# Recurrence over head pairs: the next pair's preparation and projection interleaved with this pair's matrices and scan, key norms per token, modulation on column groups

## The reference

```python
def rwkv_prep(u, p):
    r, k, v, xw, xa, xg = jnp.split(u, RW_SPLITS, axis=-1)
    w_raw = p['rw_w0'] + jnp.einsum('blde,def->bldf', jnp.tanh(xw), p['rw_w2'])
    decay = jnp.exp(-jnp.exp(-jax.nn.softplus(-w_raw) - 0.5))
    a = jax.nn.sigmoid(p['rw_a0'] + jnp.einsum('blde,def->bldf', xa, p['rw_a2']))
    kk = (k * p['rw_kk']).reshape(b_, n, RW_HEADS, RW_HEAD)
    kk = kk * lax.rsqrt(jnp.maximum(jnp.sum(kk * kk, axis=-1, keepdims=True), 1e-12))
    k_eff = k[:, :, None] * (1 + (a - 1) * p['rw_ka'])

def step(s, inp):
    sa = jnp.einsum('bhvk,bhk->bhv', s, -kk_t)
    s = s * w_t[:, :, None, :] + sa[..., None] * (kk_t * a_t)[:, :, None, :] + v_t[..., None] * k_t[:, :, None, :]
    return s, jnp.einsum('bhvk,bhk->bhv', s, r_t)
```

## Time and profile before

| | us |
|---|---|
| median of 3 runs | 4669.05 (4668.78 to 4669.14) |
| the profiled execution's own time | 4672.97 |
| its span | 4671.2 |
| busy PE / DVE / ACT | 3689.4 / 1769.3 / 776.1 |
| start of the first core stage (L696) | 222.8 |
| start of the last pair's core stage (L696) | 1319.9 |

### The profile page before, as it was taken

One profiled execution on the slowest core, in us unless ns is written; L12 is line 12 of the kernel. 1 busy time (PEld: TensorE's weight loads), 2 busy tenths in 40 slices (PEclk: granted clock), 3 DMA queues, 4 the chain that ended last, 5 costly groups with the idle time before them and its releaser, 6 DMA issues. The chain is left out here.

```text
span 4671.2 us, 51101 instructions
## 1 busy us (share of the span) xinstructions
PE 3689.4 (79%) x21012; PEld 2181.8 (47%) x21012; DVE 1769.3 (38%) x3454; ACT 776.1 (17%) x1454; POOL 60.1 (1%) x77
## 2 busy tenths in 40 slices
PE   5788778877877888886997577785978879758995
PEld 2355445544655545544443432233444444437884
DVE  2466655665563646644001300002142321332112
ACT  1223222322230211111000100001121121200011
POOL 0000000000000000000000000000000000000000
PEclk7888788888867998988998599996989999867997
DMA  3110110011101010003102599972010000026884
GB/s 130 74 51 15 64 64 35 30 64 51 45 20 51 27 48 34 27 28 153 54 36 81 197 428 428 428 316 103 39 75 36 38 36 39 36 78 259 334 330 166
DMA packets 73151, 530.80 MB, mean 114 GB/s; under 512 B 23248, under 2 KB 24656, under 8 KB 46096
## 3 DMA queue, kind: packets, MB, share of 16 engines
q1 hardware_dynamic: 66064, 503.01, 27.1%
q0 software_dynamic: 4608, 16.78, 1.0%
q10 hardware_dynamic: 2304, 8.39, 0.4%
HBM read 500.81 MB, written 27.34 MB: 113 GB/s over the span
## 5 line engine op out<-in xcount | busy, mean ns | idle before, releaser
L1740 PE MATMUL ex_ps<-ex_ring,ex_xs 128*64 128x512 f32 x1024 | 241.1, 626 | 66.7 <-DMA ex_ring<-expert_slabs_in 63.7
L2477 PEld LDWEIGHTS ge_ps<-ge_xeT,ge_ring 128*128 128x128 f32 x2048 | 233.7, 194 | 10.5 <-issue 10.5
L2477 PE MATMUL ge_ps<-ge_xeT,ge_ring 128*128 128x128 f32 x2048 | 234.0, 277 | 2.9 <-DVE ge_xeT L2535 2.9
L1974 PE MATMUL mh_ps<-mh_w,xmT 128*128 128x512 f32 x512 | 223.1, 596 | 8.6 <-ACT mh_sg L1997 8.6
L692 PE MATMUL rw_ps<-hT,rw_w 128*128 128x512 f32 (+1 forms) x560 | 218.0, 535 | 0.0
L1125 PE MATMUL sg_ps<-hTp,sg_w 128*128 128x512 f32 x384 | 180.7, 626 | 27.9 <-PEq L61 27.9
L1740 PEld LDWEIGHTS ex_ps<-ex_ring,ex_xs 128*64 128x64 f32 x1024 | 87.3, 144 | 220.0 <-issue 218.1
L1974 PEld LDWEIGHTS mh_ps<-mh_w,xmT 128*128 128x128 f32 x512 | 97.6, 191 | 133.5 <-issue 121.5
L528 PE MATMUL rw_ps<-rw_tk,cs 128*2 128x512 f32 (+2 forms) x384 | 152.6, 560 | 0.0
L692 PEld LDWEIGHTS rw_ps<-hT,rw_w 128*128 128x128 f32 x560 | 104.8, 196 | 77.0 <-issue 68.4
L1965 PE MATMUL mh_ps<-xmT,mh_w_ahead 128*128 128x512 f32 x256 | 120.7, 636 | 22.5 <-PEq L61 22.5
(11 more groups left out here) (584 smaller groups left out, 5902.4 us busy)
## 6 DMA issues: line engine op xcount, KB each, us to landing
ex_ring<-expert_slabs_in SPq DMA_DIRECT2D x96, 2048.0 KB, 17.3
ge_ring<-expert_slabs_in SPq DMA_DIRECT2D x48, 2048.0 KB, 13.1
rw_tk<-mod_w_in SPq DMA_DIRECT2D x8, 3072.0 KB, 15.4
rw_tk<-ada_in SPq DMA_DIRECT2D x8, 2048.0 KB, 9.3
mh_w_ahead<-head_slabs_in SPq DMA_DIRECT2D x8, 2048.0 KB, 10.8
mh_w<-head_slabs_in SPq DMA_DIRECT2D x8, 2048.0 KB, 10.3
rw_w<-rw_slabs_in SPq DMA_DIRECT2D x8, 1536.0 KB, 6.5
sg_w<-xbc_slabs_in SPq DMA_DIRECT2D x4, 3072.0 KB, 10.4
```

The source lines that it names most:

```text
L1740: mm = pe.matmul(ps[halves[j], bank, :], src[:, k, halves[j]], ring[:, (n + j) % RING, k, :], start=k == 0, stop=k == KC - 1)
L1974: mm = pe.matmul(ps[:, 4 + t, :], xmT[:, k, P * t:P * t + P], w[1 + n // 4][:, k, :], start=k == 0, stop=k == KC - 1)
L2477: mm = pe.matmul(ps[:, 2 + 2 * (j % 2) + n, P * f:P * f + P], w[:, k, P * f:P * f + P], xeT[:, j, k, :], start=k == 0, stop=k == KC - 1)
```

## The change

`rwkv_pair` is replaced by `one_pass(pair, nxt, core, prep)` inside `rwkv`: a single stage that does the core of `pair` and, laid between its parts on each engine, projection and preparation of `nxt = pair + 1`. It is called once with the preparation of pair 0 alone, in a loop of 7 with both, and once with the core of pair 7 alone. A short stage before them clears `xt`, `mrow` and `cond`. Everything but `outer` and the like is now held through all passes, so `by_col` shares a tile with `diag`, `by_row` with `low`, `near` is gone (its far half is copied straight to `mid`), and `t2` lies in a free part of `tk`.

- The first operation of each shift (u times the rest weight) moves from DVE to ACT (`centre`).
- Key norms: the squares are ACT's (Square with a scale). TensorE sums them with tokens as output partitions, so a 128x12 tile holds all norms of the pair. Floor, root and reciprocal work on that tile; ACT widens it to 128x768 and six matmuls turn it back (`kk_spread`).
- All copies of `wu` are ACT's, and `wu` has two banks in place of four.
- Modulation: weights come in eight slices of 128x1280 (640 KB, two loads each) into two buffers. A load waits until the slice two before was used. Each slice is multiplied in four matmuls of 320 columns with a stationary operand of 32 columns, each on its own 32 output rows, after scan steps 4 to 11.
- The 14 masks `low0` to `up6` (896 KB) leave the constants loaded at the start; the second block's heads load them beside `rope`.

```diff
-                pe.wait_ge(s.mod_in, 32)
-                pe.wait_ge(s.gates, 2)
-                for n, (lo, width, bank, m0, m1) in enumerate(((0, 512, 4, 0, 2), (0, 512, 5, 2, 3), (512, 256, 6, 2, 3))):
-                    for k in range(KC):
-                        mm = pe.matmul(ps[0:m1 - m0, bank, 0:width], cs[:, k, m0:m1], mod_weights[min(n, 1)][:, k, lo:lo + width],
-                                       start=k == 0, stop=k == KC - 1)
-                mm.then_inc(s.mod_product, 1)
...
-                dve.wait_ge(s.par_in, 16)
-                link(dve.tensor_scalar(kk[:, :], kc[:, :], col(KK), None, ALU.mult))
-                dve.tensor_tensor(e1[:, :], kk[:, :], kk[:, :], ALU.mult).then_inc(s.kk_squared, 1)
-                dve.wait_ge(s.kk_sum, 1)
-                link(dve.tensor_scalar(e1[:, CTX:NT], ps[:, 0, :], 1e-12, None, ALU.max))
-                link(dve.tensor_scalar(e1[:, 0:CTX], ps[:, 1, 0:CTX], 1e-12, None, ALU.max))
-                link(dve.reciprocal(e1[:, :], e1[:, :]))
-                dve.sem_inc(s.kk_inverse, 1)
-                dve.wait_ge(s.kk_root, 1)
-                dve.tensor_tensor(kk[:, :], kk[:, :], e1[:, :], ALU.mult).then_inc(s.kk_done, 1)
-                dve.wait_ge(s.kk_done, 1)
...
+                        for k in range(KC):
+                            if k >= 2:
+                                sp.wait_ge(s.mod_used, k - 1)
+                            sp.dma_start(mw[:, k % 2, 0:512], mod_a[0][bass.ds(pair + 4, 1), :, k, :].rearrange("a p n -> (a p) n")).then_inc(mod_in[k % 2], 16)
+                            sp.dma_start(mw[:, k % 2, 512:1280], mod_b[0][bass.ds(pair, 1), :, k, :].rearrange("a p n -> (a p) n")).then_inc(mod_in[k % 2], 16)
+                        sp.wait_ge(s.mod_done, 1)
...
+                    def kk_sums():
+                        pe.wait_ge(s.kk_squared, 1)
+                        for t in range(6):
+                            mm = pe.matmul(ps[:, 0, 2 * t:2 * t + 2], e1[:, P * t:P * t + P], halves[:, 0:P:64], start=True, stop=True)
+                        mm.then_inc(s.kk_summed, 1)
+
+                    def kk_spread():
+                        pe.wait_ge(s.norm_wide, 1)
+                        for t in range(6):
+                            out = ps[:, 3, P * t:P * t + P] if t < 2 else ps[:, 0, P * (t - 2):P * (t - 2) + P]
+                            mm = pe.matmul(out, kk[:, P * t:P * t + P], ident, start=True, stop=True)
+                        mm.then_inc(s.norm_spread, 1)
+
+                    def modulate(k):
+                        pe.wait_ge(mod_in[k % 2], 32 * (k // 2) + 32)
+                        for g in range(4):
+                            mm = pe.matmul(ps[quarter(g), MOD, 0:MW], cond[:, k, :], mw[:, k % 2, MW * g:MW * g + MW], start=k == 0, stop=k == KC - 1)
+                        mm.then_inc(s.mod_used, 1)
...
+                    if prep:
+                        pe.wait_ge(s.lora_in, 16)
+                        if core:
+                            pe.wait_ge(s.bonus_kept, 1)
+                            pe.wait_ge(s.near_kept, 3)
+                        lora_products(0)
+                    if core:
+                        keys(0)
+                    if prep:
+                        pe.wait_ge(s.w_in, 16)
+                        project_part(1, 0, 0, 4)
...
+                        if core:
+                            for d in range(2):
+                                if step > 1:
+                                    pe.wait_ge(state_ready[d], step - 1)
+                                if step + 1 < RW_NCH:
+                                    advance(d, step)
+                                if step <= 8:
+                                    inner(step - 1 + RW_CC, d, step == 1 and d == 0)
+                                if step >= RW_CC:
+                                    mm = carried(d, step)
+                        if prep:
+                            if step == 1:
+                                project_part(2, 1, 0, 3)
+                            if step == 2:
+                                project_part(2, 1, 3, 8)
+                            if step == 3:
+                                pe.wait_ge(s.filled, 1)
+                                pe.wait_ge(s.shifted_r, 1)
+                                lora_products(1)
+                        if core and step >= 4:
+                            if prep and step == 4:
+                                pe.wait_ge(s.gates, 4)
+                            modulate(step - 4)
...
+                    def centre(j, c, dst, src):
+                        act.wait_ge(s.named(f"projected{j}{c}"), 1)
+                        act.activation(dst, src, ACT.Copy, scale=rest[:, j:j + 1]).then_inc(s.named(f"centred{j}{c}"), 1)
...
+                        neighbours(1, 0, kc[:, CTX:NT], ps[:, 0, :], SEQ)
+                        neighbours(1, 1, kc[:, 0:CTX], ps[:, 3, 0:256], CTX)
+                        dve.sem_inc(s.shifted_k, 1)
+                        exponents(0)
+                        dve.wait_ge(s.kk_summed, 1)
+                        dve.tensor_scalar(norm[:, 0, :], ps[:, 0, 0:12], 1e-12, None, ALU.max).then_inc(s.norm_floor, 1)
+                    if core:
+                        keep_mr(0)
+                    if prep:
+                        dve.wait_ge(s.norm_root, 1)
+                        dve.reciprocal(norm[:, 0, :], norm[:, 1, :]).then_inc(s.norm_inverse, 1)
...
+                    if prep:
+                        dve.wait_ge(s.kk_done, 1)
+                        write_keys(0)
+                    if core:
+                        scan_step(1)
+                    if prep:
+                        neighbours(0, 0, rc[:, :], ps[:, 2, :], SEQ)
+                        dve.sem_inc(s.shifted_r, 1)
+                    if core:
+                        scan_step(2)
+                    if prep:
+                        fill(0)
+                    if core:
+                        for step in range(3, 6):
+                            scan_step(step)
+                    if prep:
+                        exponents(1)
+                    if core:
+                        for step in range(6, 9):
+                            scan_step(step)
+                    if prep:
+                        dve.wait_ge(s.gates, 4)
+                        write_keys(1)
+                    if core:
+                        for step in range(9, 11):
+                            scan_step(step)
+                        dve.wait_ge(s.mod_bias, 16 * 5)
+                        dve.wait_ge(s.mod_used, KC)
+                        dve.tensor_tensor(mrow[:, :], ps[:, MOD, 0:MW], mrow[:, :], ALU.add).then_inc(s.mod_done, 1)
+                    if prep:
+                        fill(1)
...
+        one_pass(None, 0, False, True)
+        with nc.Fori(0, PAIRS - 1) as pair:
+            one_pass(pair, pair + 1, True, True)
+        one_pass(PAIRS - 1, None, True, False)
```

972 lines of the change are left out of this document (495 added, 477 removed).

## The result

The changed kernel took 4728.77 us (median of 4 runs, 4717.19 to 4736.31), the kernel before 4668.91 in the same measurement: ratio 1.0128, 95% interval 1.0106 to 1.0149. It is slower by 60 us, where the forecast said faster by 83. The range (4530 to 4645) does not hold it.

The account below looks back on a forecast made before the run. Preparation and core ran without overlap, 156.7 us a pair, the limit shifting between DVE and TensorE. New pass 10.2 + 44.7 + 36.5 + 50.4 + 3.9 = 145.7; -77 - 16.2 + 10.2 - 0.3 = -83.3 gives 4586 us, range 4530 to 4645.

Parts of the forecast that it names:

- likeliest case: Whole kernel: preparation interleaved with the core, passes of 145.7 us, 4586 us in all; chance 0.58.
- last core: Core of pair 7 alone: the modulation's loads, `wu` and `mid` make it 10.2 us longer than 98.1.
- Start to elimination: First stretch of a pass: same work, but copies split and a table load waits; 10.2 us, before 9.7.
- `wu`, `mr`, `n`: Stretch between joining and scan: TensorE 21.9 us in a row, 3.0 for `n`, bank hand-over and copies; 26.5 us.
- The rival on the other side: From L765 to `n`: TensorE falls to 1.2 GHz, 21.9 us become 43.8; 4739 us in all; chance 0.06.
- Elimination and joining: Elimination 40.4 + 4.3 = 44.7 us; joining 10.0 us with 6 of its 22 projections left, before 19.5.
- The later first mask and the fourth projection: In the elimination: low-rank products delay the first mask 3.1 us; four projections for three add 1 us.
- Scan to end: Scan, readout to last operation: holds the next pair's preparation; DVE waits for the last slice; 50.4 us, before 20.7.
- the walk: Scan worked through step by step: modulations end at 17.0 us first and 35.0 last, slices 4.1 from use to use.
- The rival of late slices: Modulation loads in the scan need 6.5 us each, 7.2 more a pass; 4644 us in all; chance 0.11.
- Norms: Root and sums on 12 columns take under 0.5 us, hidden beside `mr`; the reciprocal's 4.95 goes with the preparation.
- Ahead of the loop: From first load to first core, 86.7 us before: clearing stage 4.5 plus a preparation alone, 66; 16.2 saved.

Follow-up runs that it names:

- e5: Changed kernel with projection products filling the hand-over around the first `wu` and the loop of 7 passes written out: 4600.31 us, ratio 0.9855 to the kernel before.
- e2: Changed kernel with its loop of 7 passes written out, no jump back: 4672.48 us, ratio 1.0007 to the kernel before.
- e10: Kernel before with only the modulation on four column groups, 32 products of 320 columns: 4662.22 us, ratio 0.9979.
- e9: Kernel before with only the key norms per token (12 columns, wide copy, six spreading products): 4668.77 us, ratio 0.9995.
- e4: Changed kernel without the modulation's loads and products; the stored row is its bias, doubled: 4654.98 us, ratio 0.9957 to the kernel before.
- e12: Changed kernel with only TensorE's order edited: one projection product ahead of the first `wu`, two behind; ScalarE's order kept: 4669.03 us, ratio 0.9991 to the kernel before.
- e1: Changed kernel with projection products around the first `wu` and ScalarE's `keep_wu(1)` ahead of the square root: 4665.27 us, ratio 0.9987 to the kernel before.

## Why the prediction was wrong

Its likeliest case was the right description of the work and the wrong description of TensorE. e5 does that same work with two edits, and its pass is the 145.7 us of the forecast: 4.2, 10.2, 43.5, 10.6, 26.5 and 50.6 where 3.9, 10.2, 44.7, 10.0, 26.5 and 50.4 stood. That this sum meets to a tenth is luck; that no term is off by more than about 1 us is not. The 14 us by which e5 lies above the forecast stand mostly in its last core, 119.7 us where 108.3 were forecast.

- **"Start to elimination. The same work ... I take 10.2 (ends 9.7 and 11.0)"** is the first step that failed: 15.2, and 4.3 more in the change of stage ahead of it. It priced the work, not where the work now stands. Before, the core's start lay in the middle of the loop's body, behind a preparation; now it is the first thing behind the jump back, and waits for its instruction list. The ends of 9.7 and 11.0 had no room for that, and no rival named it. Six times 9.3 us are 56 of the miss of 143.
- **"`wu`, `mr`, `n` ... Sum 26.5"** is the second: 35.5 on average, 39.0 where the clock stayed down. The sum of the work is right (26.5 in e5). The price came from rows at 2.4 GHz, with "in a row" put in by the text itself; it also said that the two banks cost "about 1 us at the first hand-over". That hand-over is where the clock went. 9.0 us in six passes and 12.5 in the first, 66 in all.
- **The rival on the other side**, "TensorE falls to 1.2 GHz in the stretch from L765 to `n`", named this place and gave 4739. It got 0.06, against it "with projections the clock is 1.00 throughout that stretch, and they are still there". That reading was wrong. In the rows the projections stand ahead of L765, in the joining; the stretch itself held none ("Before, nothing else stood there") and ran at 1.00 behind them:

```profile
448.70:465.00 16.30, 14.33 (x289) 13.56 (x288) 11.84 (x22) 4.76 (x7) 0.00 (x0) 1.00 0.01 2
```

  In the changed kernel eight of them moved to the far side of the first `wu`, behind the gap. As a mechanism it was only half right: it priced 21.9 us a pass and 9 came, below the 11.9 from which it was to decide; alone it would have left the kernel near the one before, as e2 shows (4672). The time of 4729 needed the jump as well. That it lies near 4739 is no confirmation.
- **Elimination and joining**: 43.9 and 10.3 for 44.7 and 10.0. The later first mask and the fourth projection are there.
- **Scan to end**: 51.2 for 50.4. The slices were the bound, as said, only in the passes where the clock of the scan was 0.82 or more: the last modulation ended at 34.3 to 35.0 us of the stretch, for 35.0 in the walk. In the other three of the six TensorE, never idle at 1.2 GHz, set the pace up to the fifth slice, one modulation each 3.5 us, and the last ended at 37.9 to 38.4. The slices took 4.3 to 5.0 us from use to use in pass 3, where 4.1 was assumed; the issue table of the end of pass 1's scan counts from each issue, and the second issue is 0.5 us behind the first (count, KB each, median us to landing):

```profile
rw_mod_w<-mod_w_in SPq DMA_DIRECT2D x2, 384.0 KB, 4.4
rw_mod_w<-ada_in SPq DMA_DIRECT2D x2, 256.0 KB, 3.7
```

  The rival of late slices priced 7.2 more a pass; it did not come. The overlap on column groups is shown by e10. The mean is near the forecast because slower slices and the clock meet a first modulation that ended up to 2.5 us earlier than the 17.0 of the walk; that is in part luck.
- **Norms**: that root and reciprocal would hide beside `mr` held. Alone in the old order they are worth nothing (e9).
- **Ahead of the loop** 21.2 saved for 19.2 (16.2 and the constants' 3.0), **last core** 16 lost for 10.2: of that 8 are the modulation, which e4 (105.5 us from first matmul to last operation, 113.5 changed) takes back.

From 4586 to 4729: 56 for the jump, 66 for the clock, 5 for the scan, 3 less in elimination and joining, 6 more in the last core, 2 less ahead of the loop, 2 less behind the last core (1.0 lost for 2.7); with the 12 us by which the profiled execution lies below its median, and the 4 by which the other one lay above, that is 142 of 143.

Left open: what starts the fall of the clock at the first `wu` when the gap is filled (it falls in every pass of e12 and in most of e1 and e5, where the stretch then takes up to 28.5 us in place of 25.2), and why, with the gap open, it comes back after 7 us in some passes and after 24 to 27 in others.

## What to carry to other kernels

When a stage is taken off the head of a loop's body, look at what each engine does first behind the jump: an engine that used to wait there hid the arrival of its instruction list, and one that now has work pays for it (9 us a pass here). When fillers are spread over a stretch, put the first of them into the first hand-over, since TensorE's clock, once down there, can stay down for the whole stretch, and the same work then takes 39 us in place of 27. And when a forecast takes "TensorE, busy throughout" from the old order, the row to check is what stands in the few microseconds ahead.
